# A hybrid decoder step on one core: the prompt's queries kept on the chip in two of four raw weight buffers, rings of heads three deep, keys, values and gate stored by partition

## What is computed

```python
k, v = split(rmsnorm(h, kv_norm) @ w_kv)            # also outputs: new_k, new_v
q, g = split(rmsnorm(h, b_norm) @ w_qg)
z = q @ k.T / sqrt(128) + bias[head]
att = where(s < t, exp(log_sigmoid(z) + sum_{s<j<t} log_sigmoid(-z[j])), 0)
h = h + ((att @ v) * silu(g)) @ w_o ; y = rmsnorm(h, final_norm)
```

## Time and profile before

| | us |
|---|---|
| median of 3 runs | 1941.75 (1940.39 to 1943.08) |
| the profiled execution: its time | 1941.25 |
| its span, first to last instruction | 1939.5 |

### The profile page before, as it was taken

One profiled execution on the slowest core, in us unless ns is written; L12 is line 12 of the kernel. 1 busy time (PEld: TensorE's weight loads), 2 busy tenths in 40 slices (PEclk: granted clock), 3 DMA queues, 4 the chain that ended last, 5 costly groups with the idle time before them and its releaser, 6 DMA issues.

```text
span 1939.5 us, 43897 instructions
## 1 busy us (share of the span) xinstructions
PE 1807.4 (93%) x18430; PEld 1539.6 (79%) x18430; DVE 1051.1 (54%) x1718; ACT 798.5 (41%) x1459; POOL 250.1 (13%) x315
## 2 busy tenths in 40 slices
PE   7999999999899999999999999999998998777897
PEld 7988999999888888799986777777776775343697
DVE  6744364453489999445445534343463444676334
ACT  4234233333466677333333323333334444555233
POOL 0300000000245555232000000000000000010132
PEclk9999999999999999999999999999999999899899
DMA  8534554554345553244889999999999999998541
GB/s 291 187 137 159 179 172 154 175 179 164 99 125 142 144 137 95 89 152 145 334 304 418 416 418 418 415 424 424 424 425 411 421 418 374 417 376 356 197 148 66
DMA packets 166968, 510.45 MB, mean 263 GB/s; under 512 B 60065, under 2 KB 99362, under 8 KB 121506
## 3 DMA queue, kind: packets, MB, share of 16 engines
q1 hardware_dynamic: 166210, 503.66, 68.9%
q10 hardware_dynamic: 576, 4.19, 0.6%
HBM read 472.86 MB, written 32.32 MB: 260 GB/s over the span
## 4 chain that ended last, share of the span: by engine, by line
PE 33%; DMA 17%; DVE 3%; ACT 2%; issue 2%; SPq 1%; DVEq 0%; ACTq 0%
DMA at_vraw<-in_cache_v 17%; PE psP L2619 8%; PE psP L2621 7%; PE psP L2620 7%; PE at_psO L2669 5%; PE at_psS L2648 3%; SPq L2032 1%; DVE wlo L2381 0%; PE psP L2714 0%; PE at_psT L2660 0%; ACT whi L2207 0%; DVE at_o_new L2536 0%; PE psP L2736 0%; DVE at_w L2469 0%; ACT at_p_w L2339 0%
## 5 line engine op out<-in xcount | busy, mean ns | idle before, releaser
L2619 PE MATMUL psP<-xhi,whi 128*128 128x320 f32 x1488 | 475.8, 320 | 2.9 <-DVE xlo L2506 1.9
L2621 PE MATMUL psP<-xhi,wlo 128*128 128x320 f32 x1488 | 460.8, 310 | 0.0
L2620 PE MATMUL psP<-xlo,whi 128*128 128x320 f32 x1488 | 460.7, 310 | 0.0
L2619 PEld LDWEIGHTS psP<-xhi,whi 128*128 128x128 f32 x1488 | 280.6, 189 | 66.6 <-issue 61.7
L2381 DVE TENSOR_TENSOR wlo<-wraw,whi 128x2048 fp32r<-128x2048 f32 x92 | 212.9, 2314 | 204.4 <-ACT whi L2207 204.1
L2207 ACT ACTIVATE whi<-wraw 128x2048 fp32r<-128x2048 f32 x92 | 176.0, 1913 | 272.8 <-PE psP L2621 271.6
L2620 PEld LDWEIGHTS psP<-xlo,whi 128*128 128x128 f32 x1488 | 280.9, 189 | 0.1
L2621 PEld LDWEIGHTS psP<-xhi,wlo 128*128 128x128 f32 x1488 | 280.6, 189 | 0.0
L132 PE MATMUL psP<-xhi,whi 128*128 128x320 f32 x704 | 218.1, 310 | 2.7 <-DVE wlo L167 2.3
L133 PE MATMUL psP<-xlo,whi 128*128 128x320 f32 x704 | 217.5, 309 | 0.0
L134 PE MATMUL psP<-xhi,wlo 128*128 128x320 f32 x704 | 217.5, 309 | 0.0
(11 more groups left out here) (372 smaller groups left out, 3073.8 us busy)
## 6 DMA issues: line engine op xcount, KB each, us to landing
wraw<-in_weights SPq DMA_DIRECT2D x156, 1024.0 KB, 6.0
at_kraw<-in_cache_k SPq DMA_DIRECT2D x96, 1024.0 KB, 10.7
at_vraw<-in_cache_v SPq DMA_DIRECT2D x94, 1024.0 KB, 10.8
at_kraw<-in_cache_k SPq DMA_DIRECT2D x64, 512.0 KB, 9.7
at_vraw<-in_cache_v SPq DMA_DIRECT2D x62, 512.0 KB, 10.5
rw_s0t<-in_s0T SPq DMA_DIRECT2D x16, 256.0 KB, 3.7
o_wkv_s<-rw_SN SPq DMA_DIRECT2D x16, 256.0 KB, 2.9
wraw<-in_weights ACTq DMA_DIRECT2D x4, 1024.0 KB, 5.8
```

Of the source, the lines that this page charges most:

```text
L2619: pe.matmul(out, wh, c_.xhi[:, kc, :], start=(kc == 0), stop=False)
L2620: pe.matmul(out, wh, c_.xlo[:, kc, :], start=False, stop=False)
L2621: last = pe.matmul(out, wl, c_.xhi[:, kc, :], start=False, stop=(kc == NM - 1))
```

## The change

The queries of the prompt no longer go to DRAM and back. DVE evacuates them (scaled as before) into `qP`, `[128, 16, 256]`, 16,384 bytes per partition, which is the place of raw buffers 2 and 3; PE reads the heads' queries there. The 4 stores of q, the 16 loads of Q, and q's waits for `stored` go away.

From chunk 20 (`RAW_PAIR`) to chunk 79 the weights use only raw buffers 0 and 1, so the load of chunk i (from 22 on) waits for the remainder of chunk i - 2, and is planned 2.6 us after that. From chunk 80 on there are four buffers again. The waits for the last head's z and turned values move from the load of chunk 82 to that of chunk 80.

The rings of K, V and of the gate are 3 deep: the loads of head h wait for `p_scored` and `p_vturned` of head h - 3, the gate load for `p_y` of head h - 3. Head loads are planned at -2.3 of a head's time in place of -2.6, gate loads at -0.6 in place of -1.2. `spill` of kk, kv (which are outputs) and g2 is laid out `[128, 16, 320]`, so a stored group is one line of 5,120 bytes per partition; the head's loads read lines of 1,024 bytes as before, now 20,480 bytes apart. The bias (16 columns) is loaded at the start into `consts`, `late` is smaller by it, and `z_n`, `w_n` lie in a part of `vec` that is no longer used.

```diff
-SPILL = [n for n in PROJ if n not in RESIDUAL] + ["s", "a"]
+SPILL = [n for n in PROJ if n not in RESIDUAL and n != "q"] + ["s", "a"]
+BY_PARTITION = ("kk", "kv", "g2")
-KRING, VRING, HRING, GRING = 2, 3, 4, 6
+KRING, VRING, HRING, GRING = 2, 3, 3, 3
+RAW_PAIR = 20
+def raw_buffer(i):
+    return i % (4 if i < RAW_PAIR or i >= first_chunk(BO) else 2)
+def raw_before(i):
+    return i - (4 if i < RAW_PAIR + 2 else 2)
...
-    return low_time(i - 4) + 2.6 + 0.01 * (i % 4)
+    return low_time(raw_before(i)) + 2.6 + 0.01 * (i % 4)
...
+        K, V = ([sb(f"p_{x}{j}", [P, SEQ]) for j in range(HRING)] for x in "kv")
+        late = sb("late", [P, AT_LATE])
+        sb("pad", [P, QC * GW - 2 * NHB * NEW + QC * GW - 2 * HRING * SEQ - AT_LATE])
+        qP = sb("p_q", [P, NHB, SEQ])
         vnew = sb("vnew", [NEW, D])
-        Q, K, V = ([sb(f"p_{x}{j}", [P, SEQ]) for j in range(HRING)] for x in "qkv")
...
             def load_chunk(i):
                 n, grp, q, g_all = parts(i)
-                sp.wait_ge(c_.wlo_ready, 4 * GW0 + i - 3)
+                sp.wait_ge(c_.wlo_ready, 4 * GW0 + (raw_before(i) if i < first_chunk(BO) else i - 4) + 1)
                 if i == first_chunk(BO):
                     Nv.wait(sp, "gate", NB - 1)
-                elif i == first_chunk(BO) + 2:
                     sp.wait_ge(p_z, NHB)
                     sp.wait_ge(p_vturned, NHB)
-                sp.dma_start(wraw[:, q], weight_chunk(c_, n, grp, q)).then_inc(c_.w_in[q], 16)
+                sp.dma_start(wraw[:, raw_buffer(i)], weight_chunk(c_, n, grp, q)).then_inc(c_.w_in[q], 16)
...
-                for i in range(first_chunk(QP) + 3, first_chunk(BO) - 8, 4):
+                for i in range(first_chunk(KP) + 3, first_chunk(BO) - 8, 4):
...
-                    dst = c_.spill[SP_I[PROJ[n]]].rearrange("m p t -> p m t")[:, 4 * grp:4 * grp + 4, :]
+                    dst = c_.spill[SP_I[PROJ[n]]][:, 4 * grp:4 * grp + 4, :]
...
-                    yield max(head_time(h, -2.6), low_time(first_chunk(BO) - 1) + 2.7)
+                    yield max(head_time(h, -2.3), low_time(first_chunk(BO) - 1) + 2.7)
...
-                    sp.dma_start(Q[j][:], c_.spill[SP_I["q"]][h][:, 0:SEQ]).then_inc(p_q_in[j], 16)
-                    sp.dma_start(K[j][:], c_.spill[SP_I["kk"]][h][:, 0:SEQ]).then_inc(p_k_in[j], 16)
-                    sp.dma_start(V[j][:], c_.spill[SP_I["kv"]][h][:, 0:SEQ]).then_inc(p_v_in[j], 16)
+                    sp.dma_start(K[j][:], c_.spill[SP_I["kk"]][:, h, 0:SEQ]).then_inc(p_k_in[j], 16)
+                    sp.dma_start(V[j][:], c_.spill[SP_I["kv"]][:, h, 0:SEQ]).then_inc(p_v_in[j], 16)
...
-                    yield max(head_time(h, -1.2), HEADS - 1.0)
+                    yield max(head_time(h, -0.6), HEADS - 1.0)
...
+                        if name == "q":
+                            dve.tensor_tensor(qP[:, k], psP[:, m, 0:SEQ], rs[:, 0:SEQ], ALU.mult).then_inc(c_.evacuated, 1)
+                            continue
                         if m == 0:
                             dve.wait_ge(c_.stored, spilled_before(n) + 16 * grp)
-                        if name == "q":
-                            dve.tensor_tensor(stage[:, m], ps, rs[:], ALU.mult).then_inc(c_.evacuated, 1)
-                            continue
...
-                    pe.wait_ge(p_q_in[j], times(h))
...
-                    pe.matmul(psA[:, 0:P], Q[j][:, 0:P], K[j][:, 0:P], start=True, stop=True)
-                    pe.matmul(psA[:, P:ZW], Q[j][:, P:SEQ], K[j][:, 0:SEQ], start=True, stop=True).then_inc(p_scored, 1)
+                    pe.matmul(psA[:, 0:P], qP[:, h, 0:P], K[j][:, 0:P], start=True, stop=True)
+                    pe.matmul(psA[:, P:ZW], qP[:, h, P:SEQ], K[j][:, 0:SEQ], start=True, stop=True).then_inc(p_scored, 1)
```

More of the change, by code:

```diff
@@ L1793 @@
 AT_COLS = AT_NEW + 2 * NEW - TS
-AT_LATE = AT_COLS - AT_BIAS
+AT_LATE = AT_COLS - AT_MASK
 def first_chunk(n):
@@ L1911, in in_weights_place @@
         zp = [sb(f"p_z{j}", [P, ZW]) for j in range(3)]
-        G = [sb(f"p_g{j}", [P, SEQ]) for j in range(GRING)]
+        G = [sb(f"p_g{j}", [P, SEQ]) for j in range(GRING - 1)]
         zadd, wp, rp, attT = (sb("p_" + x, [P, ZW]) for x in ("zadd", "w", "rc", "attT"))
@@ L1915, in in_weights_place @@
         yp = [sb(f"p_y{j}", [P, SEQ]) for j in range(2)]
-    return kN, vS, vnew, Q, K, V, late, z_n, w_n, qn, st_n, er, osn, zp, G, zadd, wp, rp, attT, vn, yp
+    return kN, vS, vnew, qP, K, V, late, qn, st_n, er, osn, zp, G, zadd, wp, rp, attT, vn, yp
 def trunk(nc, c_, a):
@@ L1932, in trunk @@
         qp = sb("qp", [P, 2, 4, 160])
+        last_g = sb("p_g_last", [P, SEQ])
         z, w = (sb(x, [P, 2, BK]) for x in ("z", "w"))
         st, osb = sb("st", [P, 2, KB, P]), sb("osb", [P, DH])
+        spent = VEC["mu0"] * NM
+        z_n, w_n = (c_.vec[:, spent + NEW * j:spent + NEW * j + NEW] for j in range(2))
         pt = sb("pt", [1, NB * NPAGE], I32)
@@ L1937, in trunk @@
         bias_of = [c_.consts[:, 8 + u:9 + u] for u in range(SHARING)] + [biasQ] * (NB - SHARING)
-        kN, vS, vnew, Q, K, V, late, z_n, w_n, qn, st_n, er, osn, zp, G, zadd, wp, rp, attT, vn, yp = c_.in_weights_place
+        kN, vS, vnew, qP, K, V, late, qn, st_n, er, osn, zp, G, zadd, wp, rp, attT, vn, yp = c_.in_weights_place
+        G = G + [last_g]
         wraw, whi, wlo, psP = c_.wraw, c_.whi, c_.wlo, c_.psP
-        bias, mask, new_mask = (late[:, x - AT_BIAS:y - AT_BIAS] for x, y in
-                                ((AT_BIAS, AT_MASK), (AT_MASK, AT_NEW), (AT_NEW, AT_COLS)))
+        bias = c_.consts[:, 8 + SHARING:8 + SHARING + NHB]
+        mask, new_mask = (late[:, x - AT_MASK:y - AT_MASK] for x, y in ((AT_MASK, AT_NEW), (AT_NEW, AT_COLS)))
         psO, psS, psT, psM = (ctx.enter_context(nc.psum_tensor("at_ps" + x, [P, 512], F32)) for x in "OSTM")
@@ L1963, in trunk @@
                         ("v", "z sp rc arg l0 l1 l2 l3 o gate")))
-        p_q_in, p_k_in, p_v_in = ([sem(f"p_{x}_in{j}") for j in range(HRING)] for x in "qkv")
+        p_k_in, p_v_in = ([sem(f"p_{x}_in{j}") for j in range(HRING)] for x in "kv")
         p_g_in = [sem(f"p_g_in{j}") for j in range(GRING)]
@@ L1977, in spilled_before @@
         def spilled_before(n):
-            return 16 * (16 + 4 * (n - QP)) + 1
+            return 16 * (16 + 4 * (n - KP)) + 1
         def times(h):
@@ L2028, in sample_part @@
             def sample_part(x):
-                return c_.spill[SP_I[x]].rearrange("m p t -> p m t")[:, :, SEQ:TOK]
+                return c_.spill[SP_I[x]][:, :, SEQ:TOK]
             def page(b, k, pg):
@@ L2106, in news @@
                 sp.wait_ge(c_.stored, spilled_before(G2))
-                sp.dma_start(late[:], a["at_fixed"][:, AT_BIAS:AT_COLS]).then_inc(late_in, 16)
+                sp.dma_start(late[:], a["at_fixed"][:, AT_MASK:AT_COLS]).then_inc(late_in, 16)
                 sp.dma_start(vS[:], sample_part("kv")).then_inc(vs_in, 16)
@@ L2127, in gates @@
                         sp.wait_ge(p_y, h - GRING + 1)
-                    elif h % 4 == 0:
+                    if h % 4 == 0:
                         sp.wait_ge(c_.stored, spilled_before(G2) + 16 * (h // 4 + 1))
-                    sp.dma_start(G[h % GRING][:], c_.spill[SP_I["g2"]][h][:, 0:SEQ]).then_inc(p_g_in[h % GRING], 16)
+                    sp.dma_start(G[h % GRING][:], c_.spill[SP_I["g2"]][:, h, 0:SEQ]).then_inc(p_g_in[h % GRING], 16)
             sp.dma_start(pt[:], a["page_table"].rearrange("(o b) n -> o (b n)", o=1)).then_inc(pt_in, 16)
-            sp.dma_start(c_.consts[:, 3:8 + SHARING], a["at_fixed"][:, AT_BIASQ:AT_BIAS]).then_inc(fixed_in, 16)
+            sp.dma_start(c_.consts[:, 3:8 + SHARING + NHB], a["at_fixed"][:, AT_BIASQ:AT_MASK]).then_inc(fixed_in, 16)
             sp.wait_ge(pt_in, 16)
@@ L2187, in heads @@
                         pool.wait_ge(c_.bank_full, heads_from)
+                        pool.wait_ge(fixed_in, 16)
                         pool.wait_ge(late_in, 16)
@@ L2206, in splits @@
                         act.wait_ge(p_low, NHB)
-                    act.activation(whi[:, i % 2], wraw[:, q], ACT.Copy).then_inc(c_.whi_ready, 1)
+                    act.activation(whi[:, i % 2], wraw[:, raw_buffer(i)], ACT.Copy).then_inc(c_.whi_ready, 1)
             def gates():
@@ L2380, in splits @@
                     dve.wait_ge(c_.whi_ready, 4 * GW0 + i + 1)
-                    dve.tensor_tensor(wlo[:, i % 2], wraw[:, q], whi[:, i % 2], ALU.subtract).then_inc(c_.wlo_ready, 1)
+                    dve.tensor_tensor(wlo[:, i % 2], wraw[:, raw_buffer(i)], whi[:, i % 2], ALU.subtract).then_inc(c_.wlo_ready, 1)
             def evacuations():
@@ L2785, in program @@
         c_.spill = [a["o_" + x] if x in ("kk", "kv") else
-                    nc.dram_tensor("spill_" + x, [NM, P, TOK], F32, kind="Internal").ap() for x in SPILL]
+                    nc.dram_tensor("spill_" + x, [P, NM, TOK] if x in BY_PARTITION else [NM, P, TOK], F32, kind="Internal").ap()
+                    for x in SPILL]
```

(6 more changed lines are left out.)

3 lines of the change are left out of this document (removed).

## The result

| | us |
|---|---|
| changed kernel, median of 20 runs | 1947.09 (1941.40 to 1950.58) |
| kernel before, beside it, median of 20 runs | 1942.05 (1935.16 to 1953.32) |
| ratio | 1.0028, 95% interval 1.0016 to 1.0040 |

The change makes the kernel slower, by 0.0028 x 1942 = 5.4 us (3.1 to 7.8). I had forecast 2.9 us less, and my range ended at 1945. Both sign and size are wrong. The profiled execution of the changed kernel spans 1944.4 us. A later run of it gave 1.0036 again.

A forecast was written before the change was run, and what follows sets the result against it. It took DMA bytes to bound the kernel from 1010 to 1675 us, nearly nothing before and little after. Terms -0.5 (up to 1610), -2.2 (queries' loads) and -0.2 (order) gave -2.9, from 1941.75 to 1938.9 us; range 1932 to 1945.

The forecast's parts named there:

- The bias loaded early and `late` smaller: Loading the bias at the start and shrinking `late` was priced at 0.
- Rival D: Slower: the two late weight loads cost their full 5.0 us, earlier savings unused; about +4, 1945.5 us; chance 0.13.
- Sum up to 1610: Stores, layout and late weight loads up to 1610 us together: -0.5 us, between -3.8 and +1.9.
- Queries not stored: Four q stores go, two of them in the full DMA stretch from 1010: -3.4 us (-3.1 to -4.8).
- Layout: Ten stores of keys, values and gate in the full stretch, in 5,120-byte lines, save 0.2 each: -2.0 us (0 to -4).
- Raw pair: Two weight loads more, for chunks 78 and 79, between 1565 and 1610: +5.0 us, 0.1 of it hidden; loads in time.
- Queries not loaded: 16 Q loads go; nine are issued before 1675 us: -2.2 us, the other seven 0 (up to -2.6).
- order: Planning K and V at -2.3 puts block 49's values ahead of head 1's loads: -0.2 us.
- Shorter rings: New SP waits are over except head 7's gate, delaying block 56's keys some 0.8 us: 0 (up to +1.3).
- rival E: SP held behind a gate or head whose forerunner is late, moving the block chain: +1.3, 1940.2 us; chance 0.05.
- rival B: Every byte counts until 1780 us and the late weight loads find room: -6.8, 1935 us; chance 0.28.
- rival C: The saved transfers were hidden anyway, PE and the fixed order setting the pace: 1941.5 us; chance 0.12.

The follow-up runs named there:

- e3_rings: Kernel before with only the rings of K, V, Q and gate at three and head and gate loads planned at -2.3 and -0.6: 0.9994.
- e7_shift256: Kernel before with consts 64 unused columns (256 bytes) wider: 0.9993.
- changed, again: The changed kernel as it is, run again beside the padded one and the kernel before: median 1946.61 us, 1.0036.
- e13: The changed kernel with 48 unused columns more in consts, so that its growth is 256 bytes: median 1934.54 us, 0.9979.
- e5: The changed kernel with the bias in a tensor of its own behind all others, loaded by its own transfer: 0.9973.
- e10: The aligned changed kernel (bias in its own tensor behind all others) run once more: 0.9986.
- e2: Kernel before with only the weights' buffers changed: two raw buffers from chunk 20, four again from chunk 80: 1.0019.
- e6: Kernel before with consts 16 unused columns (64 bytes) wider: 1.0027.
- e12: Kernel before, no offset, with pair, rings, planned times and layout together; q still goes through DRAM: 1.0022.
- e1: Kernel before with only keys, values and gate stored by partition, 128 lines of 5,120 bytes a group: 0.9991.
- e9: Kernel before with only the weight buffers (raw, high and low) moved by 64 bytes, pages on a multiple of 256: 1.0008.
- e8: Kernel before with only the page buffers moved by 64 bytes, raw weight buffers on a multiple of 256: 1.0026.

## Why the prediction was wrong

Worked out from the timelines of one trace each, in us from chunk 4's split. Kernels of one kind scatter by some 2 us at chunk 79, and by more at the end (`e3_rings` 1105.7, `e7_shift256` 1114.9, though both measured as before):

| | split 76 | split 79 | last block's values | end |
|---|---|---|---|---|
| before | 740.5 | 776.1 | 979.0 | 1110.6 |
| changed | 744.4 | 783.9 | 981.5 | 1113.1 |
| changed, again | 744.6 | 782.6 | 984.6 | 1116.6 |
| e13, padded | 737.9 | 775.5 | 974.1 | 1105.6 |
| e5, aligned | 735.2 | 775.7 | 971.3 | 1102.8 |
| e10, aligned | 739.8 | 777.7 | 973.9 | 1105.7 |
| e2, pair only | 742.1 | 779.9 | 980.2 | 1111.6 |
| e6, +64 bytes only | 747.2 | 782.4 | 987.9 | 1119.4 |

- **"The bias loaded early and `late` smaller: 0."** This is the step that failed. I priced the load and not the place: the 64 bytes that it adds to `consts` push every buffer behind it off a multiple of 256 bytes. Alone, an offset costs 5.2, 9.9 or 8.9 us (64, 128, 192 bytes); in the changed kernel, from its padded form to itself, about 11. The kernel without the offset shows that this one term turned the sign. My own sign of being wrong came, chunk 79 later than before, and none of my rivals held its cause. Rival D gives nearly the measured time, 1945.5, by another mechanism (the late weight loads at full cost with no gain before them); with the offset gone that mechanism is still in place and the kernel is faster, so D isn't the cause.
- **Sum up to 1610, -0.5.** Right where buffers are aligned: chunk 79's split came 0.4 and 0.6 us earlier and 1.6 later in e5, e13 and e10. With the offset it came 7.8 and 6.5 later.
- **Queries not stored, -3.4, and split 76 "3 to 5 us earlier".** Aligned, it came 5.3, 2.6 and 0.7 us earlier (e5, e13, e10), in the changed kernel 3.9 later.
- **Layout, -2.0.** Measured -1.7 (-4.3 to +0.8), which fits -2.0 and 0 alike. By the packet records a 5,120-byte line takes 196 ns, four of 1,280 bytes 4 x 55 = 220; (220 - 196) x 128 lines / 16 engines = 0.19 us a store, the 0.2 that I took. The 5% of the Trainium skill's rule, quoted in the prediction, would be half of that; the records say 11%. The heads' reads of 1,024 bytes take 46 ns at either spacing: 0, as priced.
- **Raw pair, +5.0 - 0.1.** Measured +3.7 (0.6 to 6.8). In e2 the distance from split 76 to split 79 grew by 2.2 us. In time: right, and chunk 22 had 4.2 us of room.
- **Queries not loaded, -2.2, order, -0.2.** Not settled. From chunk 79's split to the last block's values before took 202.9 us, e13 198.6, e5 195.6, e10 196.2, the changed kernel 197.6: 4 to 7 us less. But `e3_rings`, which still loads the queries, took 197.5, so these distances don't tell what the loads are worth.
- **Queries in all, -5.6.** The aligned change less e12 gives -4.0 - 4.3 = -8; less the sum of e1 to e3 it gives -4.8. The two differ by no more than their intervals allow, and -5.6 lies between them.
- **Shorter rings, one wait of 0.8.** The reading was wrong and its price right. SP waits for y at the gates four times, longest 6.6 us, as the waits of SP in the changed kernel from 1610 to 1780 show (line, releaser, us in total, times, longest):

```profile
SPq L2046 <- PE at_psO L2682: 46.8, 14, 8.6
SPq L2046 <- PE at_psS L2661: 28.6, 8, 10.2
SPq L2142 <- DVE at_p_y L2592: 11.0, 4, 6.6
```

  Three further waits, 6.0 us in all, are for the heads' turned values, which I had also taken for over, and one of 5.4 is for the last remainder. All of them sum up to 97.8 us. The same view before has no wait for y, and its two rows sum up to 90.7:

```profile
SPq L2032 <- PE at_psS L2648: 47.8, 11, 9.9
SPq L2032 <- PE at_psO L2669: 42.9, 13, 6.8
```

  SP waits 7 us longer in all and 15 us less for the blocks. `e3_rings` has the same wait at the gates (10.8 us, 4 times, longest 6.1) and a ratio of 0.9994. So rival E's wait happened, and no cost of it was measured (-3.7 to +1.6, which doesn't exclude E's 1.3).
- **The chain after 1675.** I read one DMA piece before its end. There are two; the earlier trace rows lack the first:

```profile
1779.94 6.54 DMA at_vraw<-in_cache_v
```

  The path thus ran through value pages for 18 of the 20 us up to 1799.5. My sum has no term there, and no run tells whether one is due.
- **The end, 0.** Right: 131.4 to 132.0 us from the last block's values to the end in all kernels of the table.

So with the addresses kept, the change gives -5.2, -2.7 and -4.1 us where my sum had -2.9 and rival B -6.8. Each is faster than before by its interval, which speaks against rival C, and -2.9 lies in all three intervals; -6.8 lies in those of e5 and e13. The other terms of the sum are thus good in total. One by one they are only as sure as said above. The kernels that beat both are `e13_after_padded`, at 0.9979 (0.9961 to 0.9997), and `e5_aligned`, at 0.9973 (0.9959 to 0.9987).

**Open.** Why misplaced rows of weights show no dearer packets (e9), and why misplaced pages show them for only 47% of the packets (e8). Whether the size of the offset counts: 5 us at 64 bytes, 10 and 9 at 128 and 192, but the intervals overlap, the packets' means are nearly equal (313.8, 313.2, 313.8 ns), and by the fit at equal clock it is 3.8, 6.3 and 4.2 us. Why 64 bytes cost about 11 us in the changed kernel and 5 in the kernel before, with packets equally long (314.1 and 313.8 ns). Why outside the full stretch, up to 900 us, the median stays at 309 ns with the offset too. And whether e12 is truly above the sum of its parts, by 3.5 us.

## What to carry to other kernels

In a stretch that the DMA engines fill, the byte at which a buffer begins is part of its price: after any edit that adds or resizes an on-chip tensor, work out where the large transfer targets now begin, and keep them on multiples of 256 bytes, with unused columns if need be. This kernel shows it for rows of 8,192 bytes; for others it is a thing to try. When a profile shows the same DMA share at fewer GB/s, look at the duration of one packet of one size before looking at the order of the work. And price every edit by what it moves, not only by what it runs: an edit at "nothing" can shift all that lies behind it.

## What the runs showed of the hardware

- Rows of 8,192 bytes written to a partition at an offset of 64, 128 or 192 bytes past a multiple of 256 took 313 to 314 ns in the mean while the engines were full, against 309.7 to 311.4 on a multiple (over 98 of 100 of these at exactly 309): 420 or 421 GB/s in place of 423 to 426, from 1250 to 1450.
- A multiple of 256 is enough: a shift by 256 bytes measured the same as none (0.9993, 0.9978 to 1.0008).
- A stored line of 1,280 bytes took 55 ns, one of 5,120 bytes 196 to 197, a read of 1,024 bytes 46 ns whether its neighbours lay 1,280 or 20,480 bytes apart. With the 309 ns of an aligned row of 8,192 bytes, all four durations lie within 1 ns of 8 ns + 0.0368 ns per byte, an estimate fitted to these numbers: about 8 ns per packet whatever its size.
